# Softmax rows of a sparse-attention block: scaled in place on GpSimd and transposed plainly, in place of products with diagonal matrices

## The reference, cut to what matters

```python
def _sparse_attend(q, ks, vs, valid):
    qg = q.reshape(B, Q, N_KV_HEADS, GQA_GROUP, HEAD_DIM)
    s = jnp.einsum('bqhgd,bqnhd->bqhgn', qg, ks).astype(jnp.float32) * (HEAD_DIM ** -0.5)
    s = jnp.where(valid[:, :, None, None, :], s, -jnp.inf)
    p = jax.nn.softmax(s, axis=-1).astype(vs.dtype)
    o = jnp.einsum('bqhgn,bqnhd->bqhgd', p, vs)
```

## Time and profile before

| what | value |
|---|---|
| median of 3 executions | 2199.44 us (2195.97 to 2200.57) |
| the profiled execution | 2196.03 us |
| its span, first to last instruction | 2194.2 us |
| PE busy | 1994.8 us, 91% |
| DVE, ACT, POOL busy | 874.2, 597.8, 466.6 us |
| prompt blocks, scores of block 0 in DVE to the last `out_low` | 647.5 to 816.6 us |
| first product of the output projection | 855.6 us |

### The profile page before, as it was taken

The page is one execution under the profiler, slowest core; times in us unless marked ns, Lnnn a source line. Parts: engine busy times, 40 slices in busy tenths (PEclk is TensorE's granted clock), DMA queues, the critical chain, the costliest instruction groups (busy, mean ns, idle before and its releaser), DMA issues.

```text
span 2194.2 us, 36231 instructions
## 1 busy us (share of the span) xinstructions
PE 1994.8 (91%) x15486; PEld 1906.1 (87%) x15486; DVE 874.2 (40%) x1228; ACT 597.8 (27%) x837; POOL 466.6 (21%) x408
## 2 busy tenths in 40 slices
PE   6999999999957677999999999999999379999996
PEld 5999999999645456899999989999998369999996
DVE  2333322543686622533332244333224653333223
ACT  2222122421214241522222133122123452122123
POOL 2211121300000063511111232111121651111120
PEclk9999999999559798999999999999999689999998
DMA  5453322251000032233332232332230123323321
GB/s 168 139 168 96 96 87 87 74 157 39 23 0 1 1 87 68 77 96 88 84 96 87 92 92 78 96 89 83 91 106 30 51 69 96 96 83 89 98 77 39
DMA packets 258364, 179.55 MB, mean 82 GB/s; under 512 B 10806, under 2 KB 254782, under 8 KB 257757
## 3 DMA queue, kind: packets, MB, share of 16 engines
q1 hardware_dynamic: 248368, 153.71, 24.0%
q10 hardware_dynamic: 7797, 11.98, 1.7%
q0 software_dynamic: 2112, 12.59, 1.6%
HBM read 169.57 MB, written 8.08 MB: 81 GB/s over the span
## 4 chain that ended last, share of the span: by engine, by line
PE 78%; DVE 6%; issue 6%; ACT 3%; POOL 3%; another core or an unknown queue 1%; DMA 1%; ACTq 0%; POOLq 0%; DVEq 0%
PE ps L770 74%; PE ps L813 2%; PE ps L905 1%; DVE iwork L1310 1%; DVE best L1307 1%; ACT w_hi L486 1%; DVE w_lo L1155 1%; POOL diag L1706 1%; DVE xf L1181 1%; POOL sum_sq L1650 1%; DVE xf L1187 1%; POOL sum_z L1648 1%; ACT xf L522 1%; POOL k_sel L1696 1%
## 5 line engine op out<-in xcount | busy, mean ns | idle before, releaser
L770 PE MATMUL ps<-xh,w_hi 128*128 128x260 f32 x3264 | 684.7, 286 | 39.3 <-ACT xh L517 17.1
L770 PE MATMUL ps<-xh,w_lo 128*128 128x260 f32 x3264 | 677.2, 284 | 0.0
L1155 DVE TENSOR_TENSOR w_lo<-w_raw,w_hi 128x2048 fp32r<-128x2048 f32 (+2 forms) x153 | 441.0, 2883 | 442.5 <-ACT w_hi L486 442.5
L770 PEld LDWEIGHTS ps<-xh,w_hi 128*128 128x128 f32 x3264 | 519.4, 190 | 45.7 <-issue 26.6
L770 PEld LDWEIGHTS ps<-xh,w_lo 128*128 128x128 f32 x3264 | 519.8, 190 | 0.7
L770 PE MATMUL ps<-xl,w_hi 128*128 128x260 f32 x3264 | 411.7, 283 | 1.3 <-POOL xl L1734 1.3
L770 PEld LDWEIGHTS ps<-xl,w_hi 128*128 128x128 f32 x3264 | 399.6, 188 | 2.0 <-POOL xl L1734 1.5
L486 ACT CAST w_hi<-w_raw 128x2048 fp32r<-128x2048 f32 (+2 forms) x153 | 282.0, 1844 | 274.1 <-PE ps L770 262.9
L770 PE MATMUL ps<-hh,w_hi 128*128 128x260 f32 x1408 | 293.0, 283 | 0.0
L770 PE MATMUL ps<-hh,w_lo 128*128 128x260 f32 x1408 | 291.4, 282 | 0.0
L1580 DVE TENSOR_TENSOR hid<-silu_g,ps 128x520 f32<-128x520 f32 x88 | 61.3, 696 | 547.4 <-ACT silu_g L683 514.8
(11 more groups left out here) (243 smaller groups left out, 1373.1 us busy)
## 6 DMA issues: line engine op xcount, KB each, us to landing
w_raw<-in_ffn_wi_dram SPq DMA_DIRECT2D x176, 512.0 KB
w_raw<-in_ffn_wo_dram SPq DMA_DIRECT2D x32, 1024.0 KB
w_raw<-in_ffn_wo_dram SPq DMA_DIRECT2D x16, 768.0 KB
w_raw<-in_attn_w_in_dram SPq DMA_DIRECT2D x8, 1024.0 KB
keys_scratch<-key_half POOLq DMA_DIRECT2D x2, 2048.0 KB, 7.9
w_raw<-in_attn_w_o_dram SPq DMA_DIRECT2D x4, 1024.0 KB
x_in<-in_x_prompt_dram ACTq DMA_DIRECT2D x1, 2048.0 KB
out_dram<-y_out ACTq DMA_DIRECT2D x4, 512.0 KB
```

The costliest lines, as they stand in the source:

```text
L770: mm = nc.tensor.matmul(ps[0:mc, bank + 2 * m + h, 0:HT], w[:, k, m, 0:mc], x(k)[:, h * HT:(h + 1) * HT], start=first and k == 0 and w is ...
L1155: nc.vector.tensor_tensor(w_lo[:, c % 2, 0:n], w_raw[:, c % 2, 0:n], w_hi[:, c % 2, 0:n].bitcast(F32), ALU.subtract).then_inc(s_lo, 1)
```

## The change

`diag` goes. POOL scales the exponentials themselves, in place, with one instruction per head over that block's keys, and PE transposes them against the constant identity. The wait of POOL on `s_tp` goes with the tile that it guarded; the wait on `s_rinv` and the signal `s_p` stay where they were.

```diff
-        diag = at("diag", [P, 2, 4, P], offset=w_off + 28672)
...
                         for r in range(4):
-                            mm = nc.tensor.matmul(ps[:, 2 + t % 2, r * P:(r + 1) * P], sc[:, B % 2, r, j * P:(j + 1) * P],
-                                                  diag[:, B % 2, r, :], start=True, stop=True)
+                            mm = nc.tensor.transpose(ps[:, 2 + t % 2, r * P:(r + 1) * P], sc[:, B % 2, r, j * P:(j + 1) * P], ident)
                         mm.then_inc(s_tp, 1)
...
                     pool.wait_ge(s_rinv, B + 1)
                     if B == 0:
                         pool.wait_ge(s_madd, NQT)
-                    if B >= 2:
-                        pool.wait_ge(s_tp, tile_base[B - 1])
-                    nc.gpsimd.tensor_tensor(diag[:, B % 2], ident.unsqueeze(1).broadcast_to([P, 4, P]),
-                                            row_inv[:, B % 2, :].unsqueeze(2).broadcast_to([P, 4, P]), ALU.mult).then_inc(s_p, 1)
+                    for r in range(4):
+                        p = sc[:, B % 2, r, 0:(i + 1) * P]
+                        x = nc.gpsimd.tensor_scalar(p, p, row_inv[:, B % 2, r:r + 1], None, ALU.mult)
+                    x.then_inc(s_p, 1)
```

## The result

The changed kernel takes **2232.73 us** (median of 4 executions, 2228.92 to 2233.2), beside 2199.75 us for the kernel before on the same chip: ratio 1.0153, 95% interval 1.0136 to 1.0169. It is slower, as forecast, but by 33 us and not by 12.8, and the time lies outside the range. Its profiled execution took 2232.49 us, with a span of 2230.7 us (before: 2194.2), +36.5. Lines in the changed kernel are one or two lower than in the earlier trace rows.

The account below looks back on a forecast made before the run. PE is busy 91%, mostly on untouched weight products; in attention, search chains or POOL's queue set the loop. -0.3 + 3.5 + 8.1 + 1.5 = +12.8 us on the median of 2199.44 gave 2212 us, range 2200 to 2222.

Parts of the forecast that it names:

- the price of one scaling: POOL's new instruction: 0.19 us plus 1.0 ns a column, 0.70 us for 512 columns; four in a row 2.62 us.
- One tensor input, so nearer the cast: Argument for POOL's scaling: one tensor input puts it nearer the cast (0.62 us) than the two-input subtraction (1.31 us).
- The later POOL end still lies before 683.4: Blocks 1 to 7: POOL would end at 683.2 instead of 681.6, before PE starts, so PE gains nothing.
- The cover: Blocks 1 to 7: PE's products wait for the search step anyway, so POOL's work before them runs beside it.
- Rival C: A slow scaling at the subtraction's rate, four costing up to 5.0 us: +28 us, 2227 us; chance 0.11.
- Block 0: First block, on the path: scaling +1.58 us, transposes and copies faster than the products; together -0.3 us.
- DVE against POOL: Blocks 1 to 7: small two-input DVE instructions take turns with POOL's scalings; +1.0 for blocks 2, 3, +0.5 for 4 to 6: +3.5 us.
- The clock: Blocks with search steps: PE's clock falls without the diagonal products, so the scores run at 1.2 GHz; +8.1 us.
- The 1.9 us for the scores of block 2: Part of the +8.1 us: scores over 512 keys at the low clock, taken as 1.9 us between 1.65 and 2.2.
- Blocks 8 to 15: Block 8 -0.5 us, then POOL's queue is the loop, three scalings +1.7, low-clock scores 0.3: sum +1.5 us.
- Blocks 12 to 15: 128 keys: scaling +0.05 us, low-clock transposes 1.09 against 1.16, so nothing; low-clock scores taken as 0.3 us.
- the value gathers keep their distance: The 16 value gathers follow POOL's last scaling at an unchanged distance, and the decode part ends with them.

Follow-up runs that it names:

- Run 4: Kernel before, with six extra POOL instructions (scalings, copy, products) on unread memory where POOL idles, to time each kind: 2199.86 us in one execution.
- run 2: Kernel before, but PE transposes plainly; POOL still builds the diagonals, which nothing reads, so division by the row sum is left out: 2198.5 us, ratio 1.0008.
- run 3: Changed kernel, but one two-input POOL instruction scales all four heads of a block, in place of four scalings with a scalar: 2219.36 us, ratio 1.0109.
- run 10: Changed kernel, but POOL scales with four two-input instructions, one a head, in place of four with a scalar: 2223.12 us, ratio 1.0106.
- Run 1: Changed kernel, but PE multiplies the scaled tile with the identity in ordinary products in place of transposes: 2240.41 us, ratio 1.0210.
- run 11: Changed kernel, but VectorE scales the exponentials, four instructions behind the reciprocal, and GpSimd only gathers: 2212.71 us, ratio 1.0056.
- run 7: Kernel before, but VectorE builds the four diagonals behind the reciprocal and GpSimd only gathers: 2190.57 us, ratio 0.9974.
- runs 9: Kernel before, with diagonals on VectorE and value gathers right behind key gathers, seven left until the padded buffers are cleared: 2196.17 us, ratio 0.9987.
- run 12: Kernel before, but diagonals built on GpSimd for blocks 0 to 8 and on VectorE for blocks 9 to 15: 2201.3 us, ratio 1.0011.

## Why the prediction was wrong

**The step that failed is the price of one scaling.** It put an instruction that the trace did not show between the cast (0.62 us) and the two-input subtraction (1.31 us for 520 columns), near the cast because it has one input. Run 4 measured 1.57 us for 512: outside both ends. "One tensor input, so nearer the cast" was an argument about the machine that no row carried. The total of four, 6.19 us, is 2.4 times the 2.62 of the sum. The sentence from the Trainium skill, GPSIMD Engine Reference, section 3.1 (769 ns for 512 elements) would have erred in the same direction; the measurement decides.

**"The later POOL end still lies before 683.4" fell with it.** The cover was 1.8 us, from the diagonal's end at 681.62 to PE's start at 683.41, and the work behind it grew by 5.15, by over 3 us too much. The prediction named the cover and stopped at the point where the product would start; it did not say what stands behind PE's wait. It was the next search product, so that DVE's chain got later too: 8.7 of the +11.1 us in blocks 1 to 6, a term that the prediction had at nothing.

**Rival C** had a dear scaling, with a price still too low (5.0 us for four), and with 2227 us came nearest. Its chance of 0.11 was too small for a price that no row had. That its total came so near is luck all the same: it had 8.1 for the clock (measured 4.8), 13 for blocks 2 to 6 and nothing for block 1 (11.1 together), and 4.8 for blocks 8 to 15, where 15.7 were lost.

**Block 0** was judged by the same loop as blocks 8 to 15, and only the price was off: +3.4 in place of -0.3, and the four scalings cost 3.6 more than the sum had. With the diagonals kept as they were (run 2) the transposes do win there, 1.3 us.

**DVE against POOL.** Right that they meet, and not far off in size: DVE's chain instructions took 2.7 us more, where the term had 3.5. What it left out stood beside it, DVE's longer waiting for PE. That POOL instructions hold DVE one instruction at a time is what run 3 against run 10 shows: 965 and 285 ns for the same `reach`, one long instruction against four short ones, with the rest of the wait moved to the instructions behind it.

**The clock** fell where the prediction said (0.72 for 1.00 from 669 to 712 us) and cost less. The 1.9 us for the scores of block 2 were never due: these stand before the first search step, and their products took 1.13 and 1.73 us in both kernels. For the scores of blocks 3 to 7 the term had 6.2 and 4.5 were measured: those of blocks 5 and 6 took 4.71 us each, partly at the lower clock, where before they took 3.98 and 5.63. Taken by themselves the transposes cost nothing on balance: run 2 has them with POOL on time, and what it loses beside the searches it wins elsewhere. Run 1 keeps the products, has fast scores and is slower. How much of the 4.8 us comes from PE's longer waits and how much from the transposes was not separated.

**Blocks 8 to 15** were rightly read as POOL's queue from block 9. Three starts between blocks 9 and 12 grew by 2.6, 2.6 and 2.3 us, about the 2.58 by which four scalings of 256 keys exceed a diagonal: the term had the right form and a price of 0.56 in it. Blocks 12 to 15, 128 keys, were put at nothing for the scaling and lost 5.1 us, near 4 x 1.31; blocks 8 to 11 lost 10.5, near 4 x 2.58.

What the prediction had right: slower, the place (nothing outside this stage changed), that PE's saved 9.5 us do not show, and that the value gathers keep their distance.

## What to carry to other kernels

When work moves to an engine on which the trace has no instance of that instruction, the price is open above the nearest rows too; run it once at an idle place before arguing from the number of its inputs. Replacing an operand that is built once a block (four 128 x 128 diagonals) by a pass over all the data makes the cost grow with the data, 512 columns a head here, while the saving on TensorE is worth only what is waited for. And where a cover is named, compare its length with the growth, and ask what is queued behind the engine that will wait: here the next step of the very chain that had been the cover. A cheaper instruction need not be less in the way: here the two-input scalings spared POOL time and held VectorE instead.

## What the runs showed of the hardware

- GpSimd's float32 product with a scalar is dearer than the product of two tensors, and two and a half times a copy by the column: 1.57 us for 512 columns, 1.09 for 432, 0.56 for 464 (run 4). With a constant scalar it is 1.40 for 480. On VectorE the scaling takes 0.47 us on average over the four sizes, on GpSimd 1.08 (run 11 and the changed kernel).
- A GpSimd product of two inputs makes a small VectorE instruction that meets it wait until it ends: `reach`, 0.18 us alone, took 3.21 us beside one of 3.60 and 2.35 beside one of 2.75 (run 3), 0.65 and 0.43 beside the short ones (run 10). Beside a product with a scalar the same instruction took 0.20 to 0.52 us (the changed kernel), and often did not wait for the end. `need<-reach`, a reduction, stayed at 0.18 us in all of them.
- Beside the sixteen search chains VectorE lost less to the products with a scalar, though they are the longest: its instructions took 40.1 us beside four with a scalar a block, 46.0 beside four of two inputs, 47.6 beside one of two inputs, and 35.1 with no GpSimd work (run 7).
- In runs 9, 11 and 12, all with VectorE's instructions in the place of GpSimd's, TensorE stood still for 5 to 7 us once between blocks 10 and 12, while GpSimd issued gathers one behind the other for all or most of it; run 7 issues them as densely and has no such stop. It is enough to turn run 12's expected gain of 6 us into nothing. Its cause was not found, and no run tried to remove it, so the 0.26% of run 7 may depend on where the stop falls.
